# Layers written out in one block with what follows, norms by token tile, convolution in three pieces

## What is computed

```python
def hybrid_layer(x, ...):
    h = rms_norm(x, g_mix)
    z = h @ w_in
    c_q, c_kv, k_rope, u2, q_nsa, kv_nsa, gate_nsa, gate_mix = jnp.split(z, SPLIT_IDX, axis=-1)
    o_a = mla_mixer(c_q, c_kv, k_rope, ...)       # latent attention, 8 heads
    o_b = conv_mixer(u2, ...)                     # GLU, causal depthwise convolution of 31 taps, layer norm, silu
    o_c = nsa_mixer(q_nsa, kv_nsa, gate_nsa, ...) # compressed, selected and window attention
    x = x + (g_a * o_a + g_b * o_b + g_c * o_c) @ w_out
    h = rms_norm(x, g_ffn)
    return x + jnp.square(jax.nn.relu(h @ w_ff1)) @ w_ff2
```

## Time and profile before

| | us |
|---|---|
| median of 3 runs | 3035.76 |
| lowest, highest | 3033.69, 3039.55 |
| the profiled execution | 3032.14 |
| its span, first to last instruction | 3030.5 |
| first layer's first product to second layer's first product | 17.20 to 601.76 |
| mod0, the second block's first product | 1185.60 |

### The profile page before, as it was taken

One profiled execution on the slowest core, in us unless ns is written; L12 is line 12 of the kernel. 1 busy time (PEld: TensorE's weight loads), 2 busy tenths in 40 slices (PEclk: granted clock), 3 DMA queues, 4 the chain that ended last, 5 costly groups with the idle time before them and its releaser, 6 DMA issues.

```text
span 3030.5 us, 55238 instructions
## 1 busy us (share of the span) xinstructions
PE 2666.9 (88%) x23300; PEld 1829.2 (60%) x23300; DVE 1306.3 (43%) x2811; ACT 605.9 (20%) x1308; POOL 488.5 (16%) x390
## 2 busy tenths in 40 slices
PE   8997799899968998999997889888898887788777
PEld 6686585477856842444686788878785533333333
DVE  2735210146351101064464344444403777777654
ACT  1231100014310000113222444333100111111111
POOL 0000000000000000000000534332000454444452
PEclk9998999999989999999998899989999999889898
DMA  4322234243223345313310000000333899999996
GB/s 187 143 108 84 111 151 155 103 178 125 98 84 134 144 159 201 126 56 139 144 79 1 2 2 2 2 3 2 143 143 125 323 421 421 421 421 422 421 421 289
DMA packets 55034, 507.10 MB, mean 167 GB/s; under 512 B 6080, under 2 KB 6080, under 8 KB 7488
## 3 DMA queue, kind: packets, MB, share of 16 engines
q0 software_dynamic: 37024, 269.12, 21.5%
q1 hardware_dynamic: 17824, 235.41, 20.2%
HBM read 503.46 MB, written 1.05 MB: 166 GB/s over the span
## 4 chain that ended last, share of the span: by engine, by line
PE 32%; DMA 11%; DVE 8%; PEld 4%; issue 2%; ACT 2%; DVEq 1%; POOL 1%; POOLq 0%; ACTq 0%; PEldq 0%; SPq 0%
PE psum L1468 29%; DMA mem<-weights,mem 10%; PEld psum L1468 4%; DVE mem L2667 3%; PE psum L1903 3%; DVE mem L2189 2%; DMA mem<-weights 1%; DVE mem L2446 0%; PE psum L1478 0%; POOL mem L2796 0%; ACT mem L2046 0%; DVEq L2465 0%; DVE mem L2628 0%; POOL mem L2718 0%; DVE mem L2595 0%
## 5 line engine op out<-in xcount | busy, mean ns | idle before, releaser
L1468 PE MATMUL psum<-mem 64*64 64x64 f32 (+6 forms) x17432 | 1055.0, 261 | 121.3 <-DMA mem<-weights 22.0
L522 PE MATMUL psum<-mem 128*128 128x256 f32 (+8 forms) x4228 | 1027.0, 412 | 25.6 <-DVE mem L1186 12.9
L1468 PEld LDWEIGHTS psum<-mem 64*64 64x64 f32 (+3 forms) x17432 | 813.6, 150 | 358.3 <-issue 237.4
L522 PEld LDWEIGHTS psum<-mem 128*128 128x128 f32 (+4 forms) x4228 | 730.1, 183 | 315.0 <-issue 227.6
L1903 PE MATMUL psum<-mem 128*128 128x512 f32 x1024 | 506.5, 654 | 134.0 <-ACT mem L2174 133.7
L1903 PEld LDWEIGHTS psum<-mem 128*128 128x128 f32 x1024 | 209.9, 210 | 429.9 <-issue 250.1
L2796 POOL DMA_INDIRECT mem<-weights,mem x256 | 308.4, 1205 | 591.0 <-PE psum L1903 295.5
L2718 POOL TENSOR_TENSOR mem<-mem 128x512 f32<-128x512 f32 (+1 forms) x112 | 162.8, 1471 | 1325.5 <-ACT mem L2023 1070.9
L2667 DVE CUSTOM_DVE_ANT_0 mem<-mem 128x1024 f32<-128x1024 f32 x256 | 307.9, 1224 | 145.2 <-DMA mem<-weights,mem 139.6
L2189 DVE TENSOR_TENSOR mem<-psum,mem 128x512 f32<-128x512 f32 (+1 forms) x224 | 150.9, 685 | 309.7 <-PE psum L1468 291.4
L2189 DVE TENSOR_TENSOR mem<-mem 128x4 f32<-128x4 f32 (+5 forms) x201 | 144.9, 729 | 105.8 <-ACTq L1959 82.7
(11 more groups left out here) (222 smaller groups left out, 1127.1 us busy)
## 6 DMA issues: line engine op xcount, KB each, us to landing
mem<-weights SPq DMA_DIRECT2D x102, 2048.0 KB, 7.3
mem<-weights SPq DMA_DIRECT2D x2, 2176.0 KB, 7.7
mem<-weights,mem POOLq DMA_INDIRECT x256, 22.2
mem<-weights SPq DMA_DIRECT2D x2, 1536.0 KB, 7.4
mem<-weights SPq DMA_DIRECT2D x3, 1024.0 KB, 9.1
mem<-weights SPq DMA_DIRECT2D x2, 1152.0 KB, 8.1
mem<-weights SPq DMA_DIRECT2D x2, 1120.0 KB, 5.0
mem<-x SPq DMA_DIRECT2D x1, 1024.0 KB, 5.8
```

The source lines that it names most:

```text
L522: ins = pe.matmul(out, lhsT, rhs, start=start, stop=stop, skip_group_check=skip)
L1468: ins = pe.matmul(out, lhsT, rhs, start=start, stop=stop, skip_group_check=skip)
```

## The change

- **Written out.** The loop over the two layers is a Python loop: waits have constants, `stand` and the register arithmetic are gone. `V = by_layer[l]`; the second layer's `g_mix` is loaded early into `second_gain`, since the vector tile is still in use when it is needed.
- **One block.** `layers_sp`, `layers_pe`, `layers_act`, `layers_v` and `layers_pool` are called at the head of the second block's functions. SyncE goes on from ff2's items to mod0 and mod1, waits for `layer_done` before ctx and mod2, and loads rows2 before q1. GpSimd computes silu of the condition. The norm of x for the second block is the layers' own (`tile_norm(1, 2, t)`), ctx's norm stands between mod1 and mod2.
- **Norms by tile.** `tile_norm` adds and sums x in halves, has its own root, and scales one tile. `normed_transposes(l, i, t)` transposes 8 blocks of one tile; tile 0 is evacuated by ScalarE (8 copies of 128 columns), tile 1 by VectorE (2 products of 512).
- **Split products.** At a layer's head cq's tile 0 is split 5 + 3 around tile 1's transposes. The out products go tile by tile, with tile 0's transposes before the last bank. ff1's first item is made in halves of 128 columns by tile. The last ff2 item goes bank by bank, with the next layer's tile 0 transposes before the last bank.
- **Convolution.** `convolve((2, 3), taps)` in three pieces: taps 0 to 14 before the compressed scores are taken, 15 to 21 after the compressed probabilities, 22 to 30 after `probabilities(l, 1)`. TensorE transposes the convolved tile before Bg1 and the normed tile before Co. ScalarE takes the variance's root between two tanh, VectorE multiplies the silu parts after the first `gated`.

```diff
@@ layers_pe
-            normed_transposes(l, 0)
+            if l == 0:
+                normed_transposes(0, 0, 0)
             pe.wait_ge(*hT_by_act.at(l, 0))
...
+            b = open_(act_ring, l, "cq")
+            for k in range(5):
+                mm(b[:, 0:384], hT[:, k, 0:P], w[:, k, :], k == 0, False)
+            normed_transposes(l, 0, 1)
+            for k in range(5, 8):
+                last = mm(b[:, 0:384], hT[:, k, 0:P], w[:, k, :], False, k == 7)
...
             outputs(l, 2, nsa_v(2))
-            channel_major(act_ring, l, "gate", hT, km_view(item(l, "Bg1"), 512), 8, 4)
             pe.wait_ge(*conv_ready.at(l))
             for t in range(TT):
                 transposes(dve_ring, l, "conv", [cacc[:, c, t * P:(t + 1) * P] for c in range(4)])
-            pe.wait_ge(*nsa_out_ready.at(l))
-            channel_major(dve_ring, l, "mix", oTn, km_view(item(l, "Co"), D), 4, 8)
+            channel_major(act_ring, l, "gate", hT, km_view(item(l, "Bg1"), 512), 8, 4)
             pe.wait_ge(*conv_normed.at(l))
...
+            pe.wait_ge(*nsa_out_ready.at(l))
+            channel_major(dve_ring, l, "mix", oTn, km_view(item(l, "Co"), D), 4, 8)
             pe.wait_ge(*conv_act_ready.at(l))
             channel_major(dve_ring, l, "mix", cvT, km_view(item(l, "Bo"), D), 4, 8)
             pe.wait_ge(*merged_ready.at(l))
...
+            for t in range(TT):
+                for half in range(2):
+                    if (t, half) == (1, 1):
+                        normed_transposes(l, 1, 0)
+                    b = open_(dve_ring, l, "out")
...
+            first_ff(0, 0)
+            normed_transposes(l, 1, 1)
+            first_ff(1, 0)
             pe.wait_ge(*hT_by_dve.at(l, 1))
-            for i in range(8):
+            for pair in range(2):
+                first_ff(pair, 1).then_inc(act_ring.full, 1)
+            for i in range(1, 8):
                 channel_major(act_ring, l, "ff1", hT, km_view(item(l, f"ff1_{i}"), 512), 8, 4)
...
+                for k, t, half in by_banks if i == 7 else by_rows:
+                    if (i, t, half, k) == (7, 1, 1, 0) and l + 1 < LAYERS:
+                        normed_transposes(l + 1, 0, 0)
@@ layers_act
             probs_copies(l, 2)
-            for c in (2, 4, 6):
+            half_tanh(l, 2, 2)
+            act.wait_ge(*ln_var_ready.at(l))
+            A(lsd, aggr[:, :, 1], ACT.Sqrt, bias=C["eps"]).then_inc(ln_root_ready.sem, 1)
+            for c in (4, 6):
                 half_tanh(l, 2, c)
...
-            roots(l, 1)
-            normed_evac(l, 1, V["g_ffn"])
+            roots(l, 1, 0)
+            normed_evac(V["g_ffn"])
+            roots(l, 1, 1)
@@ layers_v
+        def tile_norm(l, i, t, add=None):
+
+            for half in range(2):
+                cols_ = slice(half * 512, (half + 1) * 512)
+                if add is not None:
+                    add(x[:, t, cols_])
+                    v.drain()
+                v.tensor_tensor_reduce(xn[:, t, cols_], x[:, t, cols_], x[:, t, cols_], 1.0, 0.0, ALU.mult, ALU.add, npart[:, half:half + 1])
+            v.drain()
+            v.tensor_tensor(nss[:, t:t + 1], npart[:, 0:1], npart[:, 1:2], ALU.add)
             v.drain().then_inc(sumsq_ready.sem, 1)
-            v.wait_ge(*root_ready.at(l, i))
-            v.reciprocal(nrs, nsd)
-            v.drain()
-            for t in range(TT):
-                v.tensor_scalar(xn[:, t, :], x[:, t, :], nrs[:, t:t + 1], None, ALU.mult)
+            v.wait_ge(*root_ready.at(l, TT * i + t))
+            v.reciprocal(nrs[:, t:t + 1], nsd[:, t:t + 1])
+            v.drain()
+            v.tensor_scalar(xn[:, t, :], x[:, t, :], nrs[:, t:t + 1], None, ALU.mult)
             v.drain().then_inc(xn_ready.sem, 1)
...
+            convolve((2, 3), range(0, 15))
...
             v.tensor_tensor(p3, p3, bc(cgs, 2, NCMP), ALU.mult).then_inc(cmp_probs_ready.sem, 1)
+            convolve((2, 3), range(15, 22))
...
             probabilities(l, 1)
+            convolve((2, 3), range(22, CONV_W))
+            v.sem_inc(conv_ready.sem, 1)
...
-            convolve((2, 3))
-            v.drain().then_inc(conv_ready.sem, 1)
...
-            for c in range(0, 8, 2):
+            gated(l, 1, 0)
+            v.wait_ge(*conv_silu_parts.at(l))
+            v.tensor_tensor(cvT, cvT, sg, ALU.mult).then_inc(conv_act_ready.sem, 1)
+            for c in (2, 4, 6):
                 gated(l, 1, c)
@@ second block, sync
+        layers_sp(sp)
         for n, (name, count) in enumerate(ITEMS2):
+            if name == "mod2":
+                sp.wait_ge(*layer_done.at(LAYERS - 1))
+                sp.dma_start(ctxs, cin.rearrange("(t p) n -> p t n", p=P)).then_inc(ctx_landed, 16)
@@ layers_pool
+        pool.wait_ge(*cond_sig_ready.at(0))
+        pool.tensor_tensor(cs, V2["c"].rearrange("p (k s) -> p k s", s=2), csig, ALU.mult)
+        pool.drain().then_inc(cond_ready.sem, 1)
```

More of the change, by code:

```diff
@@ L755, in _ @@
-            while len(act_ring.filled["layers"]) % 4:
-                open_(act_ring, l, "pad")
-                pe.drain().then_inc(act_ring.full, 1)
-        assert len(act_ring.filled["layers"]) == 92 and len(dve_ring.filled["layers"]) == 64
-    @block.scalar
-    def _(act):
+                by_rows = [(k, t, half) for k in range(4) for t in range(TT) for half in range(2)]
+                by_banks = [(k, t, half) for t in range(TT) for half in range(2) for k in range(4)]
+                for k, t, half in by_banks if i == 7 else by_rows:
+                    if (i, t, half, k) == (7, 1, 1, 0) and l + 1 < LAYERS:
+                        normed_transposes(l + 1, 0, 0)
+                    if i == 0 and k == 0:
+                        banks.append(open_(dve_ring, l, "ff2"))
+                    last = mm(banks[2 * t + half], fT[:, 4 * i + k, t * P:(t + 1) * P],
+                              w[:, k, half * 512:(half + 1) * 512], i + k == 0, i == 7 and k == 3)
+                    if i == 7 and k == 3:
+                        last.then_inc(dve_ring.full, 1)
@@ L763, in _, with layers_act @@
+        while len(act_ring.filled["layers"]) % 4:
+            open_(act_ring, l, "pad")
+            pe.drain().then_inc(act_ring.full, 1)
+        assert len(act_ring.filled["layers"]) == ACT_LAYERS and len(dve_ring.filled["layers"]) == 64 * LAYERS
+    def layers_act(act):
         act.sem_inc(act_ring.free, 4)
         A = act.activation
-        def normed_evac(l, i, gain):
-            for pair in range(0, 4, 2):
-                b = act_ring.take(act, l, f"hT{pair}")
-                for c in range(2):
-                    last = A(hT[:, 2 * pair + c, :], b[:, c * T:(c + 1) * T], ACT.Copy, scale=gain[:, 2 * pair + c:2 * pair + c + 1])
-                last.then_inc(act_ring.free, 1)
-                act.drain()
-            act.sem_inc(hT_by_act.sem, 1)
@@ L825, in _ @@
             for c in range(0, 4, 2):
-                b = act_ring.take(act, l, "u_gate")
+                b = act_ring.take(act, "u_gate")
                 for j in range(2):
```

346 lines of the change are left out of this document (178 added, 168 removed).

## The result

| us | before | after |
|---|---|---|
| median (lowest to highest) of the comparison | 3035.56 (3033.69 to 3039.55) | 2937.81 (2937.36 to 2947.01) |
| profiled execution, its span | 3032.14, 3030.5 | 2937.36, 2935.4 |

A forecast was written before the change was run, and what follows sets the result against it. TensorE, busy 2666.9 of 3030.5 us, was taken as the bound, so its pauses had to go. Gains of 54.5 + 11.8 + 13.0 + 2 + 9.5 = 90.8 us gave 2941.3 or 2945.0; forecast 2943 us, range 2928 to 2960.

The forecast's parts named there:

- The bound: Whole kernel: TensorE busy 2666.9 of 3030.5 us, so its pauses must go; each costs twice, through slow products behind it.
- The convolution: Last gate products to out products: three pieces fit VectorE's gaps, pauses go; gain 27.2 us per layer, 54.5 in all.
- pieces too long: Rival, chance 0.07: moved convolution steps run at 0.60 instead of 0.476 us, overrunning by 7.8 us in all; 2951 us.
- The norm before the feed-forward: Out products to ff1: norm by token tile removes a 10.5 us pause; gain 5.9 us per layer, 11.8 in all.
- Loads in the open: Rival, chance 0.04: ff1_0's 128-column records pay weight loads in full, 17 us per layer, 34 in all; 2977 us.
- Between the layers: End of ff2 to end of u_gate: 47.5 us becomes 34.5, gain 13.0, bounds 11 and 14.
- The start: Kernel's beginning: the split by tile lets the first product begin earlier; gain 2 us, bounds 0 and 5.
- The joint: Joint with the second block: TensorE's 13.94 us idle before mod0 falls to 4.4; gain 9.5, bounds 5 and 10.5.
- Joint late: Rival, chance 0.06: mod2 lands late or the condition comes 5 us later; gain there 3 instead of 9.5; 2950 us.
- What was counted at nothing: Removed semaphore steps and loop register arithmetic: may shave up to 4 us off small waits, counted as 0.
- Slower: Rival, chance 0.02: TensorE gets a lower clock in the layers; mean 0.92 cancels the gain, 0.90 gives 3062 us.
- Pause kept: Rival, chance 0.03: a hidden wait keeps the convolution pause, leaving only the other terms, 36 us; 2999 us.

The follow-up runs named there:

- e1: Changed kernel with the convolution's second half in one piece again on VectorE, new order kept: mod0 starts 65.7 us later, median 3010.68 us.
- e4: Changed kernel with the convolution's second piece lengthened from 14 to 26 steps, the third cut to 6: mod0 starts 13.1 us later, median 2958.99 us.
- e5: Changed kernel with TensorE's split before the feed-forward undone (transposes behind all out banks, ff1_0 in 256 columns): mod0 starts 18.8 us later, median 2947.51 us.
- e10: Changed kernel plus the edits of e7 and e8, with a gate pair between small score products and first attention outputs: mod0 starts 8.5 us earlier, median 2934.97 us.
- e12: Changed kernel with the removed semaphore steps put back on TensorE and VectorE: mod0 starts 0.5 us later, median 2944.16 us.
- e6: Changed kernel with TensorE's order between the layers undone (last ff2 item row by row, tile 0's transposes behind): mod0 starts 13.7 us later, median 2953.91 us.
- e8: Changed kernel with x loaded as two token tiles and ScalarE's table load under that load: mod0 starts 0.3 us earlier, median 2936.66 us.
- e7: Changed kernel with the condition's sigmoid before the last layer's last roots, SyncE's norm wait moved to mod3: mod0 starts 2.4 us earlier, median 2931.07 us.
- e3: Changed kernel with both the convolution's pieces and the order behind the attention undone: mod0 starts 51.8 us later, median 2995.15 us.

## Why the prediction was right, point by point

**The bound.** TensorE's idle time in the layers was the thing to take, and 72 of 83 us came from it. The remark that a pause is paid a second time, in slow products, holds in e1, e4 and e5, but not in proportion: 1.5 us behind 30.35 in e1's gate products, 7.9 behind 6.4 in e4.

**The convolution.** 27.2 per layer forecast, 28.1 and 27.9 seen. The steps ran at 6.61/14 = 0.472 us in their new places, so "pieces too long" (0.60) fell. Forecast spares of 1.9, 0.4 and 1.6 us came out as 2.09, 2.15 and 1.74. The middle one was wider than I worked out only because TensorE lost 1.7 us in that gap to the lower clock. In e10's first layer, which is without this, VectorE idled 0.49 us there, near the 0.4 of the forecast, and TensorE did not wait; e4's first layer shows that a longer piece stops it. The wait before the out products was 1.88, not 2.31: by e12, 0.4 of it was the semaphore steps.

**The norm before the feed-forward.** 5.9 forecast, 6.9 and 8.4 seen, from the first out product to the end of ff2 without the next layer's transposes (258.8 and 258.7 us before, 251.9 and 250.3 after). The two differ by the out products, 22.56 us in the first layer and 20.87 in the second, at a lower and at full clock behind the same wait of 1.88:

```profile
838.01 20.87 PE L744 MATMUL psum<-mem 128*128 128x512 f32 x48 [1.88 <-DVEq L1242]
```

What made the term too small is the price of a record of 128 columns. From 331.31 to 334.88 pass 3.57 us for 32 of them, 0.112 each, where I took 0.126. So ff1_0's 128 records take 14.3 us and not 16.1, 1.8 less. The transposes take 0.87 us per eight from start to start instead of 1.04 (0.3 us for both groups), and the small wait of 0.2 is not there. Together that is 8.2 of the 8.4. The cause is not lower clock behind the old pause: in the kernel before only the transposes were slow (3.63 us for 16), and the products behind them had a granted clock of 1.00:

```profile
368.00:375.00 7.00, 7.00 (x34) 6.15 (x33) 0.00 (x0) 0.52 (x1) 0.00 (x0) 1.00 0.81 302
```

"Loads in the open" would have made a record 0.26. By the page "TensorE: Matmul & The Clock Gate", Part 3 (The mechanism), of the Trainium skill, in the sentence that the prediction goes by, it should have been so; the rows of 0.112 us do not agree. The same section also lets a load for the background weight buffer go ahead of running matmuls, and with that they would agree.

**Between the layers.** 13.0 forecast, 13.4 seen, split by e6.

**The start.** 2 forecast, 0.97 seen (transposes of the latents at 51.10 before and 50.13 after). I halved the transposes and the evacuation but did not look at ScalarE. In the kernel before, its table load of 1.28 us ran ahead of the wait for the sum; in the kernel after it stands behind that wait, in the chain, and the first transposes begin at 11.60 instead of 11.98. e8 takes it out again. ScalarE at the start, before, after and in e8:

```profile
3.88 1.28 ACT L777 ACT_TABLE_LOAD   x1 [3.88 <-DMA mem<-tables]
```

```profile
8.85 1.28 ACT L805 ACT_TABLE_LOAD   x1 [8.85 <-DVEq L989]
```

```profile
0.81 1.28 ACT L837 ACT_TABLE_LOAD   x1 [0.81 <-PEq L2879]
```

Without the 1.28 the gain would have been 2.25. Why the load moved behind the wait is not shown.

**The joint.** 9.5 forecast, 8.6 seen. The wait was 4.35 us against 4.4, with GpSimd's product 0.21 us instead of the 0.7 I took and the hand-overs the rest. The missing 1 us is clock: a pause of 4.35 us was still enough for the products behind it to take 30.00 us, against 29.03 before and 27.63 in e7, which has no pause. "Joint late" fell. The table load took 1.28 us and the sigmoid started 0.01 us behind it. The Trainium skill, "ScalarE: Activation LUTs", What ACT_TABLE_LOAD costs, gives the switch a drain of about the same length again; this row does not show one.

**What was counted at nothing.** The semaphore steps were worth 1.4 us, inside the "up to 4". Against it stands a cost that no term had: 1.2 us per layer between the latents and the last attention outputs, the lower clock behind the small score products (1.7) less what small waits and transposes took less (0.5).

**The rivals.** "Slower" needed 0.92 in the layers; the stretch above has 1.00, to two digits. "Pause kept" fell with the list of waits. The price of "pieces too long" was itself too low: it counted an overrun once, and e4 shows that it is paid again in slow products. The sum, 90.8 us of span against 95.1, is 4.3 short: 3.5 the norms before the feed-forward, 1.5 the convolution, 0.4 between the layers, 3.2 the second block's own spread, less 2.3 in the layers' middle, 1.0 at the start and 0.9 at the joint, within rounding. That the forecast was this near owes something to these cancelling. The bounds were added up loosely too: with the 48 that the convolution's term allows, the lowest gain is 73 and not 78; the measured gain lies far from that end.

## What to carry to other kernels

Cut work into the gaps that the trace shows on its engine, with the measured cost of a step, and leave some spare where a gap's end feeds TensorE. Here 0.49 us of spare still cost nothing (e10, first layer), while pauses of 6.4 us by an overrun brought 7.9 us of slow products with them (e4). An order and the work it waits for are priced together; the order that is right for an early result is the wrong one for a late result (e1 against e3). To read effects of a few us, compare a point in the trace behind the changed part, not the whole time, when unchanged code behind it spreads by more.

## What the runs showed that I had not expected

TensorE's clock fell in stretches in which it never waited, behind small products, in 21 of 28 layers, at 1.7 or 3.3 us each time. And the unchanged second block, from mod0 to TensorE's last product, took from 1830.7 to 1849.0 us over the 14 profiles, with two profiles of one kernel at 1837.0 and 1845.0; the medians of that kernel in two groups were 2937.81 and 2945.49. The gain of the change, 3% either way, is far above that; most of the small terms are not.
